# Reordering copies, maxima and low parts around the attention stages of a two-block transformer kernel

## The chip, the cores and the metric

The kernel runs on one core of a Trainium2 chip, in one launch. The metric is the device time of the program in microseconds (us); the time before is the median of three runs. A profile of one execution is read for everything else.

## The reference

Two transformer blocks run one after the other on x of 256 tokens by 2048 columns, everything in float32. What is computed, cut to what matters here:

```
mod = silu(c) @ w_ada + b_ada                 # six rows of 2048 (adaLN): shift, scale, gate, twice
h   = rms(x) * (1 + scale1) + shift1
aq, ak, av, gq, gf, gi, gg = split(h @ w_in)  # 7 parts of 1024 columns
attn = dilated attention, 8 heads of 128: rms norm and rope on q, k; three branches
       (window, dilation) = (128,1), (512,4), (2048,16), mixed by their softmax weights
hg   = gated linear recurrence on gq, gf, gi, chunks of 64, 8 heads
x    = x + gate1 * (concat(rms(attn), hg) @ w_out)
x    = x + gate2 * (square(relu(h2 @ w_ff1)) @ w_ff2)      # hidden 8192
# second block
q, k, v = split(rms(x) @ sb_w_qkv)            # 16 heads of 128, q and k rms normalised per head
z = q k^T / sqrt(128); a = exp(logsig(z) + suffix sums of logsig(-z)), strictly causal
x = x + (a v) @ sb_w_o
x = x + square(relu(rms(x) @ mlp_w_in)) @ mlp_w_out
```

## The kernel before

**Matrix products.** Each float32 operand is split into a high part of type float32r and a low part that holds the rest (`A_hi`, `A_lo` for activations, `w_hi`, `w_lo` for weights), and a product is three matmuls: hi by hi, hi by lo, lo by hi. Weights come in pieces of 1 MB (`raw`, four buffers). A block of weights is four pieces (called chunks in the code); one piece is 24 matmuls of 128x512 in `chunk` (L269 to L271): two halves of 128 tokens, four row tiles of 128, three products. SyncE (SP) issues the load of a piece, ScalarE (ACT) copies it to `w_hi` (`split_hi`, L255) once PE is done with the piece four before, VectorE (DVE) subtracts to get `w_lo` (`split_lo`, L259), and TensorE (PE) waits for `lo_rdy`. Three pairs of PSUM banks take the results; a pair is free again when its reader has counted up `pair_read`.

**Order.** No scheduler decides anything: each engine has its own list of work, in the order in which the Python code emits it, and the engines meet in semaphores only. The stages are interleaved by hand in steps: a step is one piece on PE, with the small work of the previous group (`at_stage`, `hg_stage`) and the group's own (`at_own`, `hg_own`) put beside it.

**First block, attention.** `proj_groups` gives two attention groups (four heads each, three blocks: q, k, v) and then two recurrence groups. `at_own` squares q and k on ACT, sums on DVE, takes the root on GpSimd (POOL, `power`, L642: `ssq` to the power -1/2, always eight columns wide), scales the rows on ACT (`norm_rows`, L746), rotates them on DVE, turns them on PE and copies them back on ACT as `qT` (L771) and `kT` (L776). In group 0 the q copy and the scaling of k fall into the same step, 11. `at_stage` works on one head every two steps: scores on PE, maxima on DVE (L1359, with the reciprocals of the head before, L1339), exponentials on ACT (L812, L813), the turn on PE (L1830), a copy on ACT (L822), the product with v on PE (L1843).

**adaLN sums.** In the same steps DVE adds up the later parts of `silu(c) @ w_ada` from a ring of four pieces in X (L1177, two pieces a step, `ada_slot`, L1386), and now and then collects a finished sum (L1162, L1164). SP issues the loads of the ring (L496) from the same queue as the weights, and waits for `ring_used`.

**Second block.** The last piece of the first MLP, the residual sum on DVE (`X`, L1617 and L1620, four blocks of 512 columns), the turns of X on PE (`mix_turn`), `A_hi` on ACT (L356) and `A_lo` on DVE (L375, `mix_steps`) and the first q, k pieces run into each other. DVE sums squares of X per block (`block_squares`, L975) and takes the root after the last block (`root_of_blocks`, L979, L433). Then four groups (`sb_group`) of four heads follow, the last three in a hardware loop; v is copied by ACT (L737) at step 0 of the group after. After the last group `tail` starts the output projection: it turns the six finished tiles of MIX (L320, five banks), and the last two (`LATE4`) come after piece 8. The wait for turned tiles is one per piece (`a_chunk`, L304; L2052 for piece 9), except that the first q piece has one more of its own (L2032).

**The middle.** Between output projection and MLP of the first block, each half of 128 tokens has its root (`last_half`, L1485), its scaled rows (`rows_half`, L1493), its turns (L402), A_hi (L415) and A_lo (L420).

Of the kernel before, what the change touches and what calls it, by code (L numbers as in the profile page):

```python
# [32 lines left out]
ALU = mybir.AluOpType  # L33
# [97 lines left out]
def build(nc, a, out):  # L131
    ctx = ExitStack()
    with ctx:
# [128 lines left out]
        def chunk(pe, B, j, pair, hi, lo, start, stop, between=None, tokens=range(T), half=None):  # L262

            pe.wait_ge(lo_rdy, 4 * B + j + 1)
            for t in tokens:
# [14 lines left out]
        def square_chunk(pe, B0, order, pos, take, between=None, tokens=range(T)):  # L280
# [3 lines left out]
            if pos == mine[0] and 0 in tokens:  # L284
                take(b % 3)
            return chunk(pe, B0 + pos // CH, pos % CH, pairs[b % 3], lambda i, t: A_hi[:, CH * k + i, P * t:P * t + P],
                         lambda i, t: A_lo[:, CH * k + i, P * t:P * t + P], pos == mine[0], pos == mine[-1], between, tokens=tokens)
# [13 lines left out]
        def a_chunk(pe, B, j, pair, turned=None, tokens=range(T)):  # L301

            if turned is not None:
                pe.wait_ge(a_lo, KT // 2 * turned + 2 * (j + 1))  # L304
            chunk(pe, B, j, pair, lambda k, t: A_hi[:, CH * j + k, P * t:P * t + P],
                  lambda k, t: A_lo[:, CH * j + k, P * t:P * t + P], j == 0, j == CH - 1, tokens=tokens)
# [306 lines left out]
        def _(pool):  # L613
# [25 lines left out]
            def power(i):  # L639

                pool.wait_ge(sum_rdy, i + 1)
                pool.tensor_tensor(rstd[:, :], ssq[:, :], mhalf[:, :], ALU.pow).then_inc(rstd_rdy, 1)  # L642

            for i in range(MIX_JOBS + 2):
                power(i)
# [3 lines left out]
            with pool.Fori(MIX_JOBS + 2, JOBS) as i:  # L649
                power(i)  # L650
# [3 lines left out]
        def _(act):  # L654
# [95 lines left out]
            def at_own(n, B0, s, by_row=False):  # L750
                steps = at_steps(n)
                if s in steps["norm"] and not by_row:
                    which = steps["norm"].index(s)
                    norm_rows(n, which, (QN, KN)[which])
# [9 lines left out]
                if s == steps["copy"][0]:  # L764
# [7 lines left out]
                    c.then_inc(pair_read[0], 1)  # L772
                if s == steps["copy"][1]:
# [7 lines left out]

            def at_stage(n, B0, s, stick):
                if s == 0:
                    act.wait_ge(chunk_done, 4 * (B0 + 3))
                    if not isinstance(n, int) or n:
                        act.wait_ge(pv_mm, 4 * n)
                    if stick:
                        from_pair(VN, 2, ACT.Copy, True).then_inc(pair_read[2], 1)
                    else:
                        act.activation(V1_heads[:, :, :, 0:HD], PS[:, 4:6, :].rearrange("p t (h d) -> p t h d", d=HD),  # L790
                                       ACT.Copy).then_inc(pair_read[2], 1)
# [1317 lines left out]
```

## Time and profile before

| | us |
|---|---|
| median of 3 runs | 2403.96 (2402.80 to 2404.01) |
| the profiled execution | 2404.46 |
| its span | 2402.7 |
| PE busy | 2327.9 (97%) |
| DVE busy | 1641.8 (68%) |
| ACT busy | 1047.6 (44%) |
| POOL busy | 51.4 (2%) |
| mean granted TensorE clock | 0.993 of full |

The span is the time from the first to the last instruction; what lies around it is the difference to the execution's own time. Busy time counts instructions that compute; an engine that waits for a semaphore is idle. All starts below are us from the span's start. Stages: start and adaLN to 140, attention of block 1 from 140 to 320, recurrence to 545, MLP 1 from 600 to 1270, second attention to 1650, MLP 2 to the end.

### The profile page before, as it was taken

The numbers are of one execution on the slowest core, as the hardware profiler recorded it, in microseconds if no ns is written. First come the engines' busy times: TensorE is split into PE (matmuls) and PEld (weight loads), VectorE is DVE, ScalarE is ACT, GpSimd is POOL, SyncE is SP. The second block draws the span as 40 slices with busy tenths as digits, with TensorE's granted clock in tenths as the row PEclk, the third lists the DMA queues.
The fourth block names the chain that finished last, engine by engine and source line by source line (L and its number), as shares of the span: only waits on it lengthen the run. The fifth ranks groups of instructions, "written<-read, shape, count | busy, mean of one in ns | idle before, by whom it ended". The sixth has DMA issues, their size and how long they took to land.

```text
span 2402.7 us, 27691 instructions
## 1 busy us (share of the span) xinstructions
PE 2327.9 (97%) x10698; PEld 1940.5 (81%) x10698; DVE 1641.8 (68%) x1349; ACT 1047.6 (44%) x922; POOL 51.4 (2%) x56
## 2 busy tenths in 40 slices
PE   4789999999999999999999999999999999999999
PEld 4677888887888888888887888878888888888887
DVE  7868989887677677665678456556666565665665
ACT  2245553435444343443444566564444343443442
POOL 1011000001000000000000000000000000000000
PEclk9989999999999999999999999999999999999999
DMA  9988987754877777666664545435566666666663
GB/s 351 369 293 319 352 316 265 265 205 142 293 254 271 263 263 277 230 228 206 212 213 167 197 145 170 158 129 168 190 222 224 211 227 212 211 230 210 213 228 123
DMA packets 258185, 553.86 MB, mean 231 GB/s; under 512 B 12281, under 2 KB 29122, under 8 KB 255426
## 3 DMA queue, kind: packets, MB, share of 16 engines
q1 hardware_dynamic: 257408, 552.72, 66.7%
q8 instruction: 48, 0.79, 0.1%
q10 hardware_dynamic: 706, 0.17, 0.0%
q14 instruction: 23, 0.19, 0.0%
HBM read 533.96 MB, written 18.87 MB: 230 GB/s over the span
## 4 chain that ended last, share of the span: by engine, by line
PE 89%; DVE 4%; DMA 2%; ACT 1%; issue 1%; DVEq 1%; POOL 1%; ACTq 0%; SPq 0%
PE PS L269 28%; PE PS L270 28%; PE PS L271 28%; DMA ada_raw<-in_w_ada_dram 2%; PE PS L1778 1%; DVE w_lo L259 1%; PE PS L1713 1%; DVE ada_acc L1177 1%; PE PS L320 1%; POOL rstd L642 1%; PE PS L1723 1%; ACT w_hi L255 1%; PE PS L1739 1%; DVE MS L1122 0%; PE PS L1843 0%
## 5 line engine op out<-in xcount | busy, mean ns | idle before, releaser
L259 DVE TENSOR_TENSOR w_lo<-raw,w_hi 128x2048 fp32r<-128x2048 f32 x392 | 897.2, 2290 | 540.7 <-ACT w_hi L255 535.5
L255 ACT ACTIVATE w_hi<-raw 128x2048 fp32r<-128x2048 f32 x392 | 751.3, 1917 | 1050.7 <-PE PS L271 1038.1
L269 PE MATMUL PS<-w_hi,A_hi 128*128 128x512 f32 x2112 | 837.9, 397 | 11.6 <-DVE A_lo L375 5.1
L270 PE MATMUL PS<-w_lo,A_hi 128*128 128x512 f32 x2112 | 826.5, 391 | 0.0
L271 PE MATMUL PS<-w_hi,A_lo 128*128 128x512 f32 x2112 | 826.4, 391 | 0.0
L269 PEld LDWEIGHTS PS<-w_hi,A_hi 128*128 128x128 f32 x2112 | 399.6, 189 | 94.1 <-issue 4.1
L271 PEld LDWEIGHTS PS<-w_hi,A_lo 128*128 128x128 f32 x2112 | 399.0, 189 | 84.4
L270 PEld LDWEIGHTS PS<-w_lo,A_hi 128*128 128x128 f32 x2112 | 399.5, 189 | 80.9 <-issue 1.0
L269 PE MATMUL PS<-w_hi,H_hi 128*128 128x512 f32 x1024 | 398.5, 389 | 0.4 <-DVE SQ L1617 0.4
L270 PE MATMUL PS<-w_lo,H_hi 128*128 128x512 f32 x1024 | 398.4, 389 | 0.0
L271 PE MATMUL PS<-w_hi,H_lo 128*128 128x512 f32 x1024 | 398.3, 389 | 0.0
L269 PEld LDWEIGHTS PS<-w_hi,H_hi 128*128 128x128 f32 x1024 | 192.3, 188 | 40.7 <-DVE SQ L1617 0.8
L271 PEld LDWEIGHTS PS<-w_hi,H_lo 128*128 128x128 f32 x1024 | 192.3, 188 | 39.9
L270 PEld LDWEIGHTS PS<-w_lo,H_hi 128*128 128x128 f32 x1024 | 192.3, 188 | 39.8
L1177 DVE SCALAR_TENSOR_TENSOR ada_acc<-X,sc,ada_acc 128x1024 f32<-128x1024 f32 x90 | 115.3, 1281 | 4.5
L1543 DVE TENSOR_TENSOR X<-X,PS 128x1024 f32<-128x1024 f32 x60 | 72.6, 1210 | 31.6 <-PE PS L271 31.6
L1543 DVE TENSOR_TENSOR ACC<-ACC,PS 128x1024 f32<-128x1024 f32 x60 | 72.6, 1210 | 28.4 <-PE PS L271 28.4
L642 POOL TENSOR_TENSOR rstd<-ssq,mhalf 128x8 f32<-128x8 f32 x20 | 44.7, 2235 | 1653.4 <-DVE ssq L433 1386.7
L1122 DVE SCALAR_TENSOR_TENSOR MS<-ada_raw,sc,MS 128x2048 f32<-128x2048 f32 x25 | 58.7, 2350 | 15.4 <-DMA ada_raw<-in_w_ada_dram 14.9
L899 ACT ACTIVATE H_hi<-SQ 128x512 fp32r<-128x512 f32 x64 | 36.9, 624 | 58.2 <-DMA SQ<-H_spill 58.2
L1713 PE MATMUL PS<-sc,ada_raw 128*128 128x1 f32 x160 | 29.0, 315 | 30.5 <-DMA ada_raw<-in_w_ada_dram 30.5
L1713 PEld LDWEIGHTS PS<-sc,ada_raw 128*128 128x128 f32 x160 | 28.9, 282 | 31.1 <-DMA ada_raw<-in_w_ada_dram 16.7
(268 smaller groups left out, 1096.9 us busy)
## 6 DMA issues: line engine op xcount, KB each, us to landing
raw<-in_w_ff_dram SPq DMA_DIRECT2D x128, 1024.0 KB, 5.3
raw<-in_mlp_w_in_dram SPq DMA_DIRECT2D x64, 1024.0 KB, 5.3
raw<-in_mlp_w_out_dram SPq DMA_DIRECT2D x64, 1024.0 KB, 5.1
raw<-in_w_in_dram SPq DMA_DIRECT2D x56, 1024.0 KB, 8.0
X<-in_w_ada_dram SPq DMA_DIRECT2D x96, 512.0 KB, 5.7
raw<-in_sb_w_qkv_dram SPq DMA_DIRECT2D x48, 1024.0 KB, 5.1
ada_raw<-in_w_ada_dram SPq DMA_DIRECT2D x32, 1024.0 KB, 9.9
raw<-in_w_out_dram SPq DMA_DIRECT2D x16, 1024.0 KB, 6.8
```

The source lines that it names most:

```text
L255: act.activation(w_hi[:, j, :, :], raw[:, j, :, :], ACT.Copy).then_inc(hi_rdy, 1)
L259: dve.tensor_tensor(w_lo[:, j, :, :], raw[:, j, :, :], w_hi[:, j, :, :].bitcast(F32), ALU.subtract).then_inc(lo_rdy, 1)
L269: pe.matmul(bank(pair + t), h, w_hi[:, j, k, :], start=first, stop=False)
L270: pe.matmul(bank(pair + t), h, w_lo[:, j, k, :], start=False, stop=False)
L271: mm = pe.matmul(bank(pair + t), l, w_hi[:, j, k, :], start=False, stop=last)
L320: mm = pe.transpose(bank(banks[pos % len(banks)], P * q, P * q + P), src[:, t, kt * P:kt * P + P], ident[:, :])
L642: pool.tensor_tensor(rstd[:, :], ssq[:, :], mhalf[:, :], ALU.pow).then_inc(rstd_rdy, 1)
L899: act.activation(of_token(H_hi, par, t), SQ_turned[:, t], ACT.Copy).then_inc(h_hi, 1)
L1122: ins = dve.scalar_tensor_tensor(out=MS[:, 1 - h, :], in0=sl, scalar=sc[:, k:k + 1], in1=MS[:, 1 - h, :], op0=ALU.mult, op1=ALU.add)
L1177: ins = dve.scalar_tensor_tensor(out=acc, in0=ada_ring[:, q % CH, :], scalar=sc[:, k:k + 1], in1=acc, op0=ALU.mult, op1=ALU.add)
L1543: dve.tensor_tensor(ac, ac, PS[:, b:b + 2, :], ALU.add).then_inc(acc_read, 1)
L1713: mm = pe.matmul(bank(6, at, at + 1), ada_raw[:, k % CH, P * c:P * c + P], sc[:, k:k + 1], start=True, stop=True)
```

## The change

Six edits, none of which changes what is computed.

- `chunk` takes `turned`: the piece is then computed two row tiles at a time, for both halves of tokens, and each two wait for their own count of `a_lo`. It is used for the first four q pieces and the first four MLP pieces of the second transformer block (`a_chunk`) and for piece 9 of the second output projection, in place of L2052.
- ACT in `at_own`: the scaling of rows (`norm_rows`) is emitted after the squares and the q copy of the step, not before.
- ACT in the second block: the v copy (`stick_v`) is emitted at step 11 of its own group, ahead of the k copy, not at step 0 of the next.
- DVE in the groups that follow an attention group: `ada_slot` of a step is emitted in the next step behind `at_stage`, not at its own step's end.
- DVE at the start of the second block: `mix_steps(0)` is emitted ahead of the low part of piece 1 and of X blocks 2 and 3, and `block_squares(1)` after the last `mix_steps`.
- POOL: `power` takes a width, 2 columns for six of the 20 roots (those over whole rows), 8 for the others.

```diff
+        def chunk(..., half=None, turned=None):
             pe.wait_ge(lo_rdy, 4 * B + j + 1)
+            if turned is not None:
+                for i in range(CH // 2):
+                    pe.wait_ge(a_lo, turned + i + 1)
+                    for t in range(T):
+                        for k in (2 * i, 2 * i + 1):
+                            h, l = hi(k, t), lo(k, t)
+                            first, last = start and k == 0, stop and k == CH - 1
+                            pe.matmul(bank(pair + t), h, w_hi[:, j, k, :], start=first, stop=False)
+                            pe.matmul(bank(pair + t), h, w_lo[:, j, k, :], start=False, stop=False)
+                            mm = pe.matmul(bank(pair + t), l, w_hi[:, j, k, :], start=False, stop=last)
+                return mm.then_inc(chunk_done, 1)
...
         def a_chunk(pe, B, j, pair, turned=None, tokens=range(T)):
-            if turned is not None:
-                pe.wait_ge(a_lo, KT // 2 * turned + 2 * (j + 1))
...
+                  turned=None if turned is None else KT // 2 * turned + 2 * j)
...
-            def power(i):
+            def power(i, w):
                 pool.wait_ge(sum_rdy, i + 1)
-                pool.tensor_tensor(rstd[:, :], ssq[:, :], mhalf[:, :], ALU.pow).then_inc(rstd_rdy, 1)
+                pool.tensor_tensor(rstd[:, 0:w], ssq[:, 0:w], mhalf[:, 0:w], ALU.pow).then_inc(rstd_rdy, 1)
+            by_token = (0, POWER_OF[1] - 1, MIX_JOBS, MIX_JOBS + 1)
             for i in range(MIX_JOBS + 2):
-                power(i)
+                power(i, T if i in by_token else 8)
...
-            with pool.Fori(MIX_JOBS + 2, JOBS) as i:
-                power(i)
+            power(MIX_JOBS + 2, T)
+            with pool.Fori(MIX_JOBS + 3, JOBS - 1) as i:
+                power(i, 8)
+            power(JOBS - 1, T)
...
             def at_own(n, B0, s, by_row=False):
                 steps = at_steps(n)
-                if s in steps["norm"] and not by_row:
-                    which = steps["norm"].index(s)
-                    norm_rows(n, which, (QN, KN)[which])
...
                         c = act.activation(heads_t(qT, i), bank(i), ACT.Copy, ...)
                     c.then_inc(pair_read[0], 1)
+                if s in steps["norm"] and not by_row:
+                    which = steps["norm"].index(s)
+                    norm_rows(n, which, (QN, KN)[which])
...
+            def stick_v(n, B0):
+                act.wait_ge(chunk_done, 4 * (B0 + 3))
+                act.wait_ge(pv_mm, 4 * n)
+                from_pair(VN, 2, ACT.Copy, True).then_inc(pair_read[2], 1)
...
+                    if s == 11:
+                        stick_v(AT_GROUPS + g, B0)
                     at_own(AT_GROUPS + g, B0, s, True)
...
                             at_stage(pi, s, False, None)
+                            if s:
+                                ada_slot(CH * B0 + s - 1)
...
-                    ada_slot(CH * B0 + s)
+                    if not i or groups[i - 1][0] == "hg" or s == CH * nb - 1:
+                        ada_slot(CH * B0 + s)
...
             for b in range(4):
                 cols = slice(NC_ * b, NC_ * (b + 1))
+                if b == 2:
+                    mix_steps(0)
                 if b in (1, 2):
                     split_lo(dve, QKV0, b - 1)
...
-                if b in (1, 2):
-                    block_squares(b - 1)
-                if b == 2:
-                    mix_steps(0)
+                if b == 1:
+                    block_squares(0)
             mix_steps(1)
...
-            for b in (2, 3):
+            for b in (1, 2, 3):
                 block_squares(b)
...
-            pe.wait_ge(a_lo, 5 * KT // 2)
...
-                square_chunk(pe, WO0, WO_ORDER, pos, take)
+                square_chunk(pe, WO0, WO_ORDER, pos, take, turned=4 * KT // 2 + len(EARLY4) if pos == WO_EARLY else None)
```

## Rows read from the trace of the kernel before

**Rows 1.** PE's waits, whole span: total us, times, longest us

```profile
PE PS L269 <- DVE A_lo L375: 5.1, 2, 2.9
PE PS L1830 <- ACT E L813: 3.2, 1, 3.2
PE PS L269 <- ACT qT L771: 2.4, 1, 2.4
PE PS L269 <- DVE A_lo L420: 2.1, 2, 1.7
PE PS L320 <- ACT V L737: 2.1, 1, 2.1
PE PS L1843 <- ACT AM L819: 1.8, 3, 0.6
PE PS L1811 <- issue: 1.4, 1, 1.4
PE PS L1824 <- DVE E L1349: 1.2, 3, 0.4
```

**Rows 2.** Windows: length, busy us of PE, PEld, DVE, ACT, POOL, clock, DMA

```profile
176.15:181.70 5.55, 5.55 (x24) 4.57 (x25) 5.35 (x6) 2.67 (x2) 0.00 (x0) 1.00 0.91 313
223.08:230.20 7.12, 7.12 (x27) 5.76 (x26) 6.92 (x5) 1.82 (x2) 0.00 (x0) 0.76 0.94 317
1594.26:1603.98 9.72, 9.72 (x48) 8.59 (x48) 7.25 (x17) 8.64 (x17) 0.00 (x0) 0.82 0.32 110
1659.31:1666.50 7.19, 7.19 (x24) 5.74 (x25) 2.29 (x1) 0.78 (x1) 0.00 (x0) 0.76 0.40 126
```

**Rows 3.** Timeline of ACT, step 11 of attention group 0: start, us, what, idle before

```profile
172.77 2.18 ACT L746 ACTIVATE KN<-PS,rstd 128x128 f32<-128x128 f32 x8 [3.38 <-POOL rstd L642]
174.78 1.32 ACT L771 ACTIVATE qT<-PS,w_cols 128x512 f32<-128x512 f32 x2
```

**Rows 4.** Timeline of DVE, then its groups from 176 to 323 (busy, mean ns, idle)

```profile
207.00 1.22 DVE L1297 TENSOR_REDUCE ssq<-QN 128x8 f32<-128x1024 f32 x1 [1.78 <-ACT QN L735]
217.99 2.67 DVE L1177 SCALAR_TENSOR_TENSOR ada_acc<-X,sc,ada_acc 128x1024 f32<-128x1024 f32 x2
...
L1359 DVE CUSTOM_DVE_ANT_0 E<-PS,maskadd 128x128 f32<-128x128 f32 (+1 forms) x16 | 5.1, 356 | 0.7 <-issue 0.5
```

**Rows 5.** SP's waits from 140 to 330, then a low part and its use

```profile
SPq L496 <- DVE ada_acc L1177: 127.3, 53, 6.9
...
256.59 2.29 DVE L259 TENSOR_TENSOR w_lo<-raw,w_hi 128x2048 fp32r<-128x2048 f32 x1
...
267.52 0.58 PE L269 MATMUL PS<-w_hi,A_hi 128*128 128x512 f32 x1
```

**Rows 6.** Timeline of POOL and DVE: smallest memset, roots, low part

```profile
1.38 0.10 POOL L621 MEMSET mhalf<- 128x8 f32 x1
...
577.77 2.28 DVE L259 TENSOR_TENSOR w_lo<-raw,w_hi 128x2048 fp32r<-128x2048 f32 x1
577.93 3.61 POOL L642 TENSOR_TENSOR rstd<-ssq,mhalf 128x8 f32<-128x8 f32 x1 [11.34 <-DVE ssq L1485]
...
1305.15 1.64 POOL L642 TENSOR_TENSOR rstd<-ssq,mhalf 128x8 f32<-128x8 f32 x1 [711.33 <-DVE ssq L433]
```

**Rows 7.** Timeline of ACT and DVE, start of the second block

```profile
1274.94 1.57 ACT L356 ACTIVATE A_hi<-PS,colB 128x256 fp32r<-128x256 f32 x4 [4.58 <-PE PS L320]
...
1282.68 1.66 DVE L375 SCALAR_TENSOR_TENSOR A_lo<-PS,colB,A_hi 128x256 fp32r<-128x256 f32 x4
...
1306.90 8.89 DVE L259 TENSOR_TENSOR w_lo<-raw,w_hi 128x2048 fp32r<-128x2048 f32 x4
```

**Rows 8.** Timeline of DVE, tail of the second attention and output projection

```profile
1592.98 2.29 DVE L259 TENSOR_TENSOR w_lo<-raw,w_hi 128x2048 fp32r<-128x2048 f32 x1 [5.17 <-ACT w_hi L255]
1595.80 4.79 DVE L375 SCALAR_TENSOR_TENSOR A_lo<-PS,one_c,A_hi 128x256 fp32r<-128x256 f32 x12 [0.52 <-ACT A_hi L356]
...
1657.60 1.66 DVE L375 SCALAR_TENSOR_TENSOR A_lo<-PS,one_c,A_hi 128x256 fp32r<-128x256 f32 x4 [3.17 <-ACT A_hi L356]
```

More of the change, by code:

```diff
@@ L260, in split_lo, with chunk @@
                               ALU.subtract).then_inc(lo_rdy, 1)
-        def chunk(pe, B, j, pair, hi, lo, start, stop, between=None, tokens=range(T), half=None):
+        def chunk(pe, B, j, pair, hi, lo, start, stop, between=None, tokens=range(T), half=None, turned=None):
             pe.wait_ge(lo_rdy, 4 * B + j + 1)
+            if turned is not None:
[9 more added lines that the diff above has]
+                return mm.then_inc(chunk_done, 1)
             for t in tokens:
@@ L278, in chunk, with square_chunk @@
             return mm
-        def square_chunk(pe, B0, order, pos, take, between=None, tokens=range(T)):
+        def square_chunk(pe, B0, order, pos, take, between=None, tokens=range(T), turned=None):
             b, k = order[pos]
@@ L286, in square_chunk @@
             return chunk(pe, B0 + pos // CH, pos % CH, pairs[b % 3], lambda i, t: A_hi[:, CH * k + i, P * t:P * t + P],
-                         lambda i, t: A_lo[:, CH * k + i, P * t:P * t + P], pos == mine[0], pos == mine[-1], between, tokens=tokens)
+                         lambda i, t: A_lo[:, CH * k + i, P * t:P * t + P], pos == mine[0], pos == mine[-1], between, tokens=tokens, turned=turned)
         def last_of(order, b):
@@ L301, in a_chunk @@
         def a_chunk(pe, B, j, pair, turned=None, tokens=range(T)):
-            if turned is not None:
-                pe.wait_ge(a_lo, KT // 2 * turned + 2 * (j + 1))
             chunk(pe, B, j, pair, lambda k, t: A_hi[:, CH * j + k, P * t:P * t + P],
-                  lambda k, t: A_lo[:, CH * j + k, P * t:P * t + P], j == 0, j == CH - 1, tokens=tokens)
+                  lambda k, t: A_lo[:, CH * j + k, P * t:P * t + P], j == 0, j == CH - 1, tokens=tokens,
+                  turned=None if turned is None else KT // 2 * turned + 2 * j)
         def turn_pe(pe, n, src, steps=ALL, first=0, banks=WIDE):
@@ L780, in _ @@
             AMf = AM[:, :, :, :].rearrange("p r h s -> p (r h s)")
+            def stick_v(n, B0):
+                act.wait_ge(chunk_done, 4 * (B0 + 3))
+                act.wait_ge(pv_mm, 4 * n)
+                from_pair(VN, 2, ACT.Copy, True).then_inc(pair_read[2], 1)
             def at_stage(n, B0, s, stick):
-                if s == 0:
+                if s == 0 and not stick:
                     act.wait_ge(chunk_done, 4 * (B0 + 3))
-                    if not isinstance(n, int) or n:
+                    if n:
                         act.wait_ge(pv_mm, 4 * n)
[L787 to L791, printed above, removed]
+                    act.activation(V1_heads[:, :, :, 0:HD], PS[:, 4:6, :].rearrange("p t (h d) -> p t h d", d=HD),
+                                   ACT.Copy).then_inc(pair_read[2], 1)
                 if not stick and s >= 4 and s % 2 == 0 and s <= 2 * GH + 2:
```

## The prediction

> **What bounds the kernel.** I read the busy shares first: PE (TensorE) is busy for 97% of the span, so only two things can be won: time in which PE stands still, and time in which it runs at its lower clock. Eight entries of the list of PE's waits lie in the stages that the change touches [rows 1]. Three of them (5.1, 3.2 and 2.4 us) carry most. The stage windows then show what a wait costs a second time: after three of them TensorE's granted clock falls to 1.2 GHz for some microseconds, and a block of 24 matmuls takes 7.12 and 7.19 us (mean clock 0.76) where it takes 5.55 us at 2.4 GHz [rows 2]. That is 1.6 us a time; a third such row, at 1284.6, reads the same and is not shown. So a removed wait of 3 us is worth 4.6. Last I read each wait back in order of time on the engine that ends it [rows 3 to 8].
>
> **q copied before the k rows are normalised.** In the first attention group ACT normalises k (2.18 us, held by the root until 172.77) and only then copies q at 174.78 [rows 3]. The copy frees the PSUM pair of PE's next piece, which waits 2.4 us [rows 1]. q was turned five microseconds earlier, so after the change the copy lies in the 3.38 us in which ACT sits idle before the k rows, and costs nothing; the k rows keep their time. PE needs the turned k only after its next piece (5.4 us later), and DVE is done with it 1.5 us after ACT. Gain 2.4; no new wait follows.
>
> **Maxima before the adaLN additions.** Before a head's maxima DVE makes two additions, 2.67 us, as at 217.99 [rows 4]. The wait of 3.2 us for the exponentials of head 2 hangs on a longer chain: maxima of head 1, exponentials, squares of q, their sum on DVE, the root, the q rows, their rotation, a low part, the additions, the maxima of head 2. Two pairs of additions leave it: the earlier one (2.1 us) moves into the 1.78 us in which DVE waits for the squares before 207.00 [rows 4], worth 1.7; the later one gives 2.67. Head 2 is ready 4.4 earlier; PE, 2.4 earlier by the q copy, then waits 3.2 + 2.4 - 4.4 = 1.2. Gain 2.0, and the 1.6 of the slow block, since the stop of 2.4 that ends at 176.15 is followed by a block at clock 1.00 [rows 2]. What the additions pass: the collecting of finished sums falls behind odd steps, where no maxima stand, and keeps its place; the low part of each step no longer waits behind the additions of its own step but behind those of the last, so the work between two low parts is the same. SP waits for these very additions (53 times in this stretch) before it issues the next adaLN pieces, and the weight pieces stand behind them [rows 5]; they come 0.8 later per head, the maxima's own length, while PE takes a low part 8.64 us after it is ready at the tightest place (end 258.88, use 267.52) [rows 5]. The cover holds. If DVE had to wait for scores, it would break, but before the 16 instructions of eight heads' maxima it waited 0.7 us in all [rows 4]. Stage: 2.4 + 2.0 + 1.6 = 6.0; bounds 2.4 and 7.6.
>
> **Narrower root.** Six of 20 roots shrink from 8 to 2 columns. No row has a two-column root: from 0.10 us (the smallest memset) to the 1.64 of the wide one; by columns 0.4, which I take as the nearest [rows 6]. Only two matter. The root at 577.93 takes 3.61 us: it started 0.16 after a low part, and ends 1.5 after that one does (580.05), so POOL seems shut out until then. It then gates the scaled rows at 581.58, whose chain (rows, low part, half-turn's low part) ends PE's 1.7 us wait, the larger of the two of L420 [rows 1]. Narrow, it ends before DVE is free at 580.7: gain 0.8 (0 if width costs nothing). The Trainium skill, page SBUF — State Buffer, section "SBUF: two separate sides", says that VectorE and GpSimd hold their shared port pair as an exclusive lock for a whole instruction. By that rule the 2 us before the low part's end cannot be won whatever the width, and the trace agrees (3.61 against 1.64); had the whole 3.61 scaled, the root alone would end 2.7 earlier, yet DVE's own work would still cap the gain at 0.9.
>
> **Boundary to the second block.** PE waits 2.9 us of the 5.1 for the first block's A_lo, which DVE starts at 1282.68, though A_hi of block 0 is ready at 1276.5 [rows 7]. Before it stand a low part, two X operations and two pairs of squares. Moved ahead: A_lo 1276.4 to 1278.1, low part to 1280.4, X blocks 2 and 3 to 1282.9 and 1285.5, A_lo of block 1 to 1287.2 (1288.7 before). PE starts at 1281.4 instead of 1284.6, needs no slow block, ends its piece at 1286.9, and now waits 0.3 for A_lo of block 1 before it turns block 2: 2.9 + 1.6 - 0.3 = 4.2. What is late next: three pairs of squares (4.9 us instead of 3.2) and the root now stand ahead of the low part that begins at 1306.90. By the same sums A_lo of block 3 ends at 1296.7, squares 1301.7, root 1302.9, the low part 1305.2, PE's use 1305.6 (1309.88 - 4.2 = 1305.7). It just fits; with an unchanged root it is 0.8 late. So 4.2, bounds 3.0 and 4.9.
>
> **v copied first.** In the loop over groups the v copy (1.27 us) moves into ACT's wait for the turned k, and k comes 0.35 later; both have a whole piece to spare, and the loop's remaining waits (1.8 and 1.2) hang on DVE and stay [rows 1]. Only the tail gains. There PE waits for k (1.4) and then for v (2.1) [rows 1]. The second goes, the first grows to 1.8. But A_lo, which releases the sixth turn and the next piece, starts at 1595.80 behind a low part that ends 1595.27, which itself follows k's copy [rows 8]: it does not move, and PE gets the wait back after five turns. Left are what the slow clock costs here (mean 0.82 over 9.72 us, 1.75) [rows 2] less a likely return of it: I take 0.5, bounds -0.9 and 1.2.
>
> **Half chunks.** The ninth piece of the output projection waits 2.2 us for both A_lo steps, 1.66 us together [rows 8]; after the change for the first, 0.8 less. The wait is then 1.4, short of what lowered the clock, so 1.6 more: 2.4, bounds 0.8 and 2.5. In the first q piece the finer wait does nothing, as the old one (L2032) stays, and in the last MLP none of PE's waits stood; 24 matmuls in another order cost the same.
>
> **Sum.** 6.0 + 0.8 + 4.2 + 0.5 + 2.4 = 13.9. The profiled execution took 2404.46 us (span 2402.7), 0.5 above the median 2403.96. Against it: 2404.46 - 13.9 = 2390.6; the median of runs I set at 2390.4.
>
> **Rivals.** (1) The clock still falls: the remaining stops at 218, 1595 and 1658 each keep a slow block. For it: a fall came after only 2.2 us at 1657. Against: none after 2.4 at 174 [rows 2]. Price 1.6 + 1.6 + 1.7 = 4.9: 2395.3. (2) DVE takes back what the first stage gives: from 176 to 323 it has hardly any slack, and PE now runs 6 us earlier against it. Against: the 8.64 us of cover and DVE's own waits for ACT. Price 6.0: 2396.4. Both: 2399.7, as one slow block is in both. (3) The other side: SP's queue. If DVE comes to a head's maxima before PE has scored, it waits with the additions behind it, SP with the adaLN loads, and weights behind those. At five steps of each of two groups this costs up to a pair of additions, 26.7 us; it decides once 8.64 is used up: 18.1 lost, with two slow blocks 21.3, 2411.7. Against it stands the 0.7 us of [rows 4]. (4) The change doesn't do what it says where the narrow root costs as much as the wide one and v first gives nothing: 0.8 + 0.5 + 0.8, 2392.5, inside the forecast's own range.
>
> **Numbers.** Forecast 0.70, own range 2386.5 to 2395 (the bounds above, not all at one end); (1) alone 0.13, (2) alone 0.09, both 0.04, (3) 0.04. Range 2387 to 2397.5: the upper end takes in (1) and (2) alone. 0.2% is 4.8 us, about what a measurement of this kernel tells from no change: faster below 2399.2. So faster 0.92, same 0.04, slower 0.04.
>
> **What would show it.** No wait of PE for qT; the wait for E of head 2 near 1.2 us, with its block at full clock; A_lo of block 0 before 1279 less the shift, and a wait of under 0.5 before the turn of block 2; no gap before the first k piece; the V wait gone, replaced by one inside the tail's turns; 1.4 before the ninth output piece. The prediction is wrong if low parts reach PE late between 170 and 560, or if the granted clock has as many falls as before.

## The result, and the profile after

The changed kernel takes 2390.5 us, median of 4 runs (2387.74 to 2390.72), against 2403.64 us before on the same chip: ratio 0.9944, 95% interval 0.993 to 0.9959. Forecast were 2390.4 us and a range of 2387 to 2397.5. The profiled execution took 2390.71 us, span 2388.7.

The list of PE's waits comes first, whole span (total us, times, longest us), without the rows of 4.9 us and more, which all lie in the start. Its rows answer to [rows 1]:

```profile
...
PE PS L330 <- DVE A_lo L385: 2.0, 1, 2.0
PE PS L280 <- DVE A_lo L388: 1.9, 1, 1.9
PE PS L1863 <- ACT AM L834: 1.9, 3, 0.6
PE PS L1831 <- issue: 1.7, 1, 1.7
PE PS L272 <- DVE A_lo L385: 1.5, 1, 1.5
...
PE PS L280 <- DVE A_lo L430: 1.2, 2, 0.7
PE PS L1844 <- DVE E L1366: 1.2, 3, 0.4
PE PS L1850 <- ACT E L828: 1.1, 1, 1.1
```

The waits for qT and for V are gone, the one for E at head 2 fell from 3.2 to 1.1, the one before the ninth output piece (L272) to 1.5, and the larger of the two of L430 from 1.7 to 0.7. The first row shown is new: it stands inside the tail's turns. The row marked issue, a wait for which the profile shows no cause, is the tail's wait at the scores, which the prediction puts down to k; it was 1.4 [rows 1]. The row of L388 was there before, in the start, and is not among [rows 1].

The windows of the blocks behind four of these places (same columns as [rows 2]; the clock is the third number from the end):

```profile
217.97:223.52 5.55, 5.55 (x28) 4.59 (x26) 5.18 (x5) 1.82 (x2) 0.00 (x0) 1.00 0.75 244
1273.77:1279.32 5.55, 5.55 (x27) 4.41 (x25) 5.28 (x8) 3.22 (x5) 0.00 (x0) 1.00 0.58 189
1582.39:1593.30 10.91, 8.84 (x39) 6.92 (x38) 7.80 (x17) 7.48 (x14) 0.00 (x0) 0.84 0.30 98
1646.96:1652.51 5.55, 5.55 (x25) 4.59 (x26) 2.93 (x3) 1.48 (x1) 0.00 (x0) 1.00 0.14 33
```

Three of the four slow blocks of before run at 2.4 GHz now; in the tail the clock still falls.

ACT in step 11 of group 0, answering to [rows 3], shows q copied ahead of the k rows:

```profile
168.70 1.25 ACT L781 ACTIVATE qT<-PS,w_cols 128x512 f32<-128x512 f32 x2
172.18 2.18 ACT L759 ACTIVATE KN<-PS,rstd 128x128 f32<-128x128 f32 x8 [2.23 <-POOL rstd L652]
```

DVE at the boundary and in the tail, answering to [rows 7, 8]:

```profile
1268.68 1.66 DVE L385 SCALAR_TENSOR_TENSOR A_lo<-PS,colB,A_hi 128x256 fp32r<-128x256 f32 x4
...
1287.40 1.66 DVE L385 SCALAR_TENSOR_TENSOR A_lo<-PS,colB,A_hi 128x256 fp32r<-128x256 f32 x4 [1.50 <-ACT A_hi L366]
...
1295.31 0.17 DVE L1653 COPY row_r<-rstd 128x2 f32<-128x2 f32 x1 [0.81 <-POOL rstd L652]
1295.38 8.89 DVE L259 TENSOR_TENSOR w_lo<-raw,w_hi 128x2048 fp32r<-128x2048 f32 x4
...
1581.33 2.29 DVE L259 TENSOR_TENSOR w_lo<-raw,w_hi 128x2048 fp32r<-128x2048 f32 x1 [5.46 <-ACT w_hi L255]
1583.77 4.79 DVE L385 SCALAR_TENSOR_TENSOR A_lo<-PS,one_c,A_hi 128x256 fp32r<-128x256 f32 x12
```

And the roots on POOL, with the low part on DVE that the first of them meets, answering to [rows 6]:

```profile
571.06 2.28 DVE L259 TENSOR_TENSOR w_lo<-raw,w_hi 128x2048 fp32r<-128x2048 f32 x1
...
571.22 2.67 POOL L652 TENSOR_TENSOR rstd<-ssq,mhalf 128x2 f32<-128x2 f32 x1 [12.28 <-DVE ssq L1505]
...
1294.57 0.70 POOL L652 TENSOR_TENSOR rstd<-ssq,mhalf 128x2 f32<-128x2 f32 x1 [708.40 <-DVE ssq L443]
1305.73 3.69 POOL L652 TENSOR_TENSOR rstd<-ssq,mhalf 128x8 f32<-128x8 f32 x1 [10.46 <-DVE ssq L443]
```

**The drift.** For a change of 13 us in small parts a list of waits is coarse, so the traces are set side by side in another way. PE works through 392 weight pieces of 24 matmuls each, in the same order in every kernel here. The start of a piece in one trace less its start in the trace of after is the drift, and where the drift changes, time was lost or won. The table gives, for each trace, the drift at piece 8, and then its change from stretch to stretch, in us: the copy of q (pieces 8 to 14), heads 0 to 2 (14 to 22), the root (22 to 190), the boundary (190 to 206), the loop over groups (206 to 241), its last steps (241 to 247), the tail (247 to 256), the rest; then the sum without the start.

```
kernel                  start |  8-14  14-22  22-190  190-206  206-241  241-247  247-256  256-391 | sum
before                   0.59 |  2.73   3.37    0.99     4.28    -0.02    -0.01    -0.29     2.35 | 13.42
e1_q_undone             -3.01 |  4.27  -1.64    0.00     0.05    -0.04    -0.01     0.18     0.01 |  2.83
e2_ada_undone           -0.50 |  0.00   6.13   -0.01     0.03    -0.07    -0.01     0.16     0.02 |  6.25
e3_roots_wide            1.24 |  0.00   0.00    0.94     0.97    -0.02     0.00    -1.43     0.02 |  0.49
e4_boundary_undone      -3.16 |  0.02  -0.03   -0.01     4.13    -0.11    -0.03    -1.40     0.01 |  2.59
e5_v_late               -2.29 |  0.01  -0.03    0.03     0.04     0.00    -0.03     0.35    -0.01 |  0.37
e6_piece9_whole         -2.00 |  0.01   0.01    0.00     0.05    -0.08    -0.02     0.03     0.72 |  0.72
e7_tail_first           -0.67 |  0.01  -0.06    0.03     0.03     0.06     0.56    -0.59     0.01 |  0.05
e8_three_orders          1.28 |  0.02  -0.03    0.01     0.07    11.82    -0.26    -0.58     0.01 | 11.05
e9_subtract_ahead        0.05 |  0.01   0.01    0.00     0.09    -1.76    -0.87    -1.43     0.00 | -3.95
e10_head0_ahead         -1.44 |  0.00   0.01    0.04     0.05    -3.81    -0.85    -1.43     0.00 | -6.00
e11_all_orders          -0.11 |  0.00   0.01    0.04     0.05    -3.75    -0.61    -2.35     0.01 | -6.59
e12_same_again          -1.62 |  0.00   0.00   -0.01     0.09    -0.03     0.02     0.10     0.00 |  0.17
```

A stretch that an edit does not touch repeats to 0.1 us. Two things do not repeat: the start, before piece 8, whose drift lies anywhere in 4.4 us from one execution to the next, and falls of the clock, 1.4 to 1.7 us each. The runs' times carry both, so the single edits are read from the drift and the times only bear them out.

### The profile page after: what moved, and what is told of

Read it like the earlier page. It is cut to its first block, busy times and chain, and to the rows that moved or that the text cites. A ratio compares the mean times of both kernels' runs of the same rounds, so it can differ in the third digit from the quotient of the medians.

```text
span 2388.7 us, 27685 instructions
## 1 busy us (share of the span) xinstructions
PE 2324.8 (97%) x10698; PEld 1937.2 (81%) x10698; DVE 1642.0 (69%) x1349; ACT 1047.8 (44%) x922; POOL 47.8 (2%) x56
## 4 chain that ended last, share of the span: by engine, by line
PE 90%; DVE 4%; DMA 2%; ACT 1%; DVEq 1%; issue 1%; POOL 0%; ACTq 0%; SPq 0%
PE PS L280 27%; PE PS L282 27%; PE PS L281 27%; DMA ada_raw<-in_w_ada_dram 2%; PE PS L1798 1%; DVE w_lo L259 1%; PE PS L1733 1%; PE PS L272 1%; PE PS L274 1%; PE PS L273 1%; PE PS L330 1%; DVE ada_acc L1194 1%; ACT w_hi L255 1%; PE PS L1743 1%; PE PS L1759 0%
## 5 line engine op out<-in xcount | busy, mean ns | idle before, releaser
L280 PE MATMUL PS<-w_hi,A_hi 128*128 128x512 f32 x2040 | 809.2, 397 | 3.1 <-DVE A_lo L388 1.9
L282 PE MATMUL PS<-w_hi,A_lo 128*128 128x512 f32 x2040 | 798.2, 391 | 0.0
L281 PE MATMUL PS<-w_lo,A_hi 128*128 128x512 f32 x2040 | 797.7, 391 | 0.0
L280 PEld LDWEIGHTS PS<-w_hi,A_hi 128*128 128x128 f32 x2040 | 385.9, 189 | 82.6 <-DVE A_lo L388 2.0
L282 PEld LDWEIGHTS PS<-w_hi,A_lo 128*128 128x128 f32 x2040 | 385.0, 189 | 81.5
L281 PEld LDWEIGHTS PS<-w_lo,A_hi 128*128 128x128 f32 x2040 | 386.0, 189 | 78.4 <-issue 1.0
L652 POOL TENSOR_TENSOR rstd<-ssq,mhalf 128x8 f32<-128x8 f32 (+1 forms) x20 | 41.1, 2056 | 1642.0 <-DVE ssq L443 1377.9
```

The source lines that it names most:

```text
L280: pe.matmul(bank(pair + t), h, w_hi[:, j, k, :], start=first, stop=False)
L281: pe.matmul(bank(pair + t), h, w_lo[:, j, k, :], start=False, stop=False)
L282: mm = pe.matmul(bank(pair + t), l, w_hi[:, j, k, :], start=False, stop=last)
L652: pool.tensor_tensor(rstd[:, 0:w], ssq[:, 0:w], mhalf[:, 0:w], ALU.pow).then_inc(rstd_rdy, 1)
```

## The experiments

Ratios are to the kernel before, with 95% intervals; each kernel is the changed one with the edit shown.

**1. The q copy behind the k rows again.**

```diff
+                if s in steps["norm"] and not by_row:
+                    which = steps["norm"].index(s)
+                    norm_rows(n, which, (QN, KN)[which])
                 if s == steps["square"][0]:
...
                     c.then_inc(pair_read[0], 1)
-                if s in steps["norm"] and not by_row:
-                    which = steps["norm"].index(s)
-                    norm_rows(n, which, (QN, KN)[which])
```

> The changed kernel (2390.5 us) with the q copy behind the normalisation of k again in the first attention stage; all else of the change stays. Interplay theory (mine): the order of q sets when head 0 of the first group starts, but from head 2 on DVE's maxima and collections decide. At piece 12 of the drift the 2.6 us come back, of which head 2's wait (1.1 us in the changed kernel, 3.0 before) gives back what it can spare: net 1.2 us lost, 2391.7, and the clock fall at 127.6 stays away or is moved. Additive rival: q's 2.4 to 2.6 us are lost in full: 2393.0, and if the clock falls again as before, 2394.6.

Measured 2391.13 us, 0.9949 (0.9929 to 0.9968); one of its four runs, 6063 us, lies far outside, and without it the median is 2390.45. PE's waits from 160 to 240 us and the window behind them:

```profile
PE PS L280 <- ACT qT L784: 2.4, 1, 2.4
```

```profile
172.53:179.72 7.19, 7.19 (x25) 5.79 (x26) 6.99 (x6) 2.65 (x2) 0.00 (x0) 0.76 0.86 292
```

The wait for qT is back and the one for E at head 2 is gone: PE comes there late enough. From piece to piece (12, 13, 17, 19) the drift changes by +2.57, +1.69, -0.35 and -1.31. The 1.69 are the clock, which fell right behind this wait, so the order of q by itself is worth 2.57 - 0.35 - 1.31 = 0.9, near the 1.2 of the interplay; the additive rival's 2.4 to 2.6 are out. The fall itself neither theory foresaw: in the kernel before, PE waited as long at this place and the block behind ran at clock 1.00 [rows 2]. The fall at 127.6 that the expectation names is one of the start's, which every trace has.

**2. The maxima behind the additions again.**

```diff
                             at_stage(pi, s, False, None)
-                            if s:
-                                ada_slot(CH * B0 + s - 1)
...
-                    if not i or groups[i - 1][0] == "hg" or s == CH * nb - 1:
-                        ada_slot(CH * B0 + s)
+                    ada_slot(CH * B0 + s)
```

> The changed kernel with only the order of the maxima undone: in the first attention stage the pieces of ada's sums stand ahead of the next head's work on DVE again. Interplay theory: head 2 of the first group is then late whatever q does, so q's gain is lost with it (its wait at head 2 grows by what the wait at head 0 gave) and the clock falls as before: 2.1 + 2.6 + 1.6 = about 6.0 us lost, 2396.5; the drift against the kernel before then falls by 2.6 at weight piece 12 and climbs back at piece 19. Additive rival: only its own 2.0 and the clock's 1.6 are lost: 2394.1.

Measured 2395.07 us, 0.9968 (0.9957 to 0.9978). PE's waits from 170 to 240 us, and the window behind the longest:

```profile
PE PS L1847 <- ACT E L828: 5.5, 3, 3.8
```

```profile
221.98:229.17 7.19, 7.19 (x28) 5.77 (x27) 6.97 (x5) 1.82 (x2) 0.00 (x0) 0.76 0.98 328
```

All of the first stage's gain is lost, 6.13 us against 6.10 (2.73 + 3.37) for both edits undone. With DVE late at three heads (the drift rises by 1.42, 0.34 and 2.74, then 1.62 for the clock) the early q copy is worth nothing. The additive rival (3.6) is out.

**3. All roots over eight columns.**

```diff
-                power(i, T if i in by_token else 8)
+                power(i, 8)
...
-            power(MIX_JOBS + 2, T)
+            power(MIX_JOBS + 2, 8)
...
-            power(JOBS - 1, T)
+            power(JOBS - 1, 8)
```

> The changed kernel with all roots of GpSimd over eight columns again. Theory: the loss is the 0.9 us of the root at 571 us (piece 74 of the drift) and nothing elsewhere, since the boundary's own root at 1294.6 us (0.70 us now) is followed by work that the DVE has in hand only in part: 0 to 0.9 there. 2391.4, up to 2392.3. Rival: the span of a root is set by how it meets the low parts on the shared port, so the width is worth nothing on the path: 2390.5.

Measured 2391.0 us, 0.995 (0.9933 to 0.9967). PE's waits from 500 to 1310 us, two of the roots on POOL, and the tail's window in this trace:

```profile
PE PS L280 <- DVE A_lo L430: 2.2, 2, 1.7
PE PS L280 <- DVE w_lo L259: 0.9, 1, 0.9
```

```profile
572.46 3.62 POOL L652 TENSOR_TENSOR rstd<-ssq,mhalf 128x8 f32<-128x8 f32 x1 [11.34 <-DVE ssq L1505]
...
1296.78 1.64 POOL L652 TENSOR_TENSOR rstd<-ssq,mhalf 128x8 f32<-128x8 f32 x1 [708.44 <-DVE ssq L443]
```

```profile
1585.52:1595.01 9.49, 7.33 (x40) 5.88 (x38) 7.80 (x17) 7.48 (x14) 0.00 (x0) 1.00 0.33 112
```

The width is worth 0.94 at the middle root and 0.97 at the boundary, 1.9 in all, where the reordered squares leave no room for a wide root. That is just over the 0 to 0.9 that the theory gave the boundary, and the rival's nothing is out. And where the clock fell in the tail of the changed kernel (0.84 over 10.91 us) it did not here (1.00 over 9.49 us), with the same work and the same 2.0 us of waiting: 1.4 us to the good that have nothing to do with roots.

**4. The boundary's order undone.**

```diff
-                if b == 2:
-                    mix_steps(0)
                 if b in (1, 2):
                     split_lo(dve, QKV0, b - 1)
...
-                if b == 1:
-                    block_squares(0)
+                if b in (1, 2):
+                    block_squares(b - 1)
+                if b == 2:
+                    mix_steps(0)
...
-            for b in (1, 2, 3):
+            for b in (2, 3):
```

> The changed kernel with the order of the turn and the squares at the boundary to the second block undone. Theory: the terms are independent of all else, so 4.3 us come back at weight pieces 200 and 201, with the clock fall at 1284.7: 2394.8. Rival: the narrower root and the earlier v have moved the place, and less than 3 us come back: below 2393.5.

Measured 2391.7 us, 0.9956 (0.9939 to 0.9972). PE's waits from 1260 to 1290 us and the window behind:

```profile
PE PS L272 <- DVE A_lo L385: 2.7, 1, 2.7
```

```profile
1273.57:1280.75 7.18, 7.18 (x25) 5.71 (x26) 6.39 (x7) 0.22 (x1) 0.00 (x0) 0.76 0.01 2
```

4.13 us come back at this place (2.98 + 1.38 - 0.23), of 4.28. The finer waits of the q pieces were not undone by themselves; what is left for them here is 0.15. The time rose by only 1.2: the start was 3.2 earlier than in the trace of after, and the clock did not fall in the tail (-1.40). Read by its time alone this run would have spoken for the rival.

**5. v copied late again.**

```diff
                 at_stage(n, B0, 0, stick)          # in tail
+                if stick:
+                    stick_v(n, B0)
...
+                        if s == 0:
+                            stick_v(AT_GROUPS + g - 1, B0 - 3)
                         at_stage(AT_GROUPS + g - 1, B0 - 3, s, True)
-                    if s == 11:
-                        stick_v(AT_GROUPS + g, B0)
```

> The changed kernel with v's copy back at the head of the next stage (and of the tail's turn) in the second block's attention; all else of the change stays. Theory: v first does nothing that the path sees; in the tail the wait at E's use of v (1.9 us before) comes back in place of the waits inside the turns, so against the changed kernel the drift at pieces 248 and 249 shows between -0.3 and +0.6 us and the clock falls or not in either: 2390.2 to 2391.0. Rival (my forecast's step): v first was worth 0.5 us, with up to 0.5 more per stage in the loop: 2391.0 to 2392.5.

Measured 2389.43 us, 0.9944 (0.993 to 0.9957). PE's waits from 1570 to 1600 us:

```profile
PE PS L330 <- ACT V L750: 2.1, 1, 2.1
PE PS L1833 <- issue: 1.4, 1, 1.4
PE PS L1846 <- DVE E L1368: 0.6, 1, 0.6
```

The wait for V is back in place of the one inside the turns, and the loop's stretches do not move (0.00, -0.03). In the tail this trace is 0.35 longer than after, while the trace of before was 0.29 shorter; a fall of the clock lies in all three, at another point of the work each time. The edit is worth nothing that can be told from zero.

**6. The ninth output piece waits for both low parts again.**

```diff
+            pe.wait_ge(a_lo, 5 * KT // 2)
             def mlp_turn(b):
...
-                square_chunk(pe, WO0, WO_ORDER, pos, take, turned=4 * KT // 2 + len(EARLY4) if pos == WO_EARLY else None)
+                square_chunk(pe, WO0, WO_ORDER, pos, take)
```

> The changed kernel with the half chunk undone: the tensor engine waits for the low parts of both last turned blocks before piece 9 of the output projection. Theory: 0.8 us of waiting comes back at piece 257 of the drift (0.70 measured there in the change), and with a wait that long (2.6 us) the clock falls again, 1.6 us more: 2392.9. Rival: the two are not bound together, the clock falls or doesn't whatever this wait is, as it did at 1585 us in the changed kernel and not in two of its variants: 0.8 us alone, 2391.3.

Measured 2389.96 us, 0.9942 (0.9929 to 0.9956). PE's waits from 1640 to 1660 us and the window behind:

```profile
PE PS L280 <- DVE A_lo L385: 2.2, 1, 2.2
```

```profile
1645.65:1651.20 5.55, 5.55 (x24) 4.62 (x25) 2.29 (x1) 0.79 (x1) 0.00 (x0) 1.00 0.22 52
```

The wait is as long as before, and the clock stays up: 0.72 us, the rival's answer. The 1.6 us of clock that the change won here are not bound to this wait.

**7. The tail's last weight piece split behind the turned blocks.** The last group is written out, so that it can differ.

```diff
             def tail(...):   # ScalarE; VectorE alike with split_lo
                 turn_act(act, turn, g, steps=steps, banks=TAIL)
+                if stick:
+                    split_hi(act, B, CH - 1)
...
-                    split_hi(act, B0 + s // CH + 1, s % CH)
+                    if s < 11 or not last:
+                        split_hi(act, B0 + s // CH + 1, s % CH)
...
-            with act.Fori(1, SB_GROUPS) as g:
+            with act.Fori(1, SB_GROUPS - 1) as g:
                 sb_group(g, False)
+            sb_group(SB_GROUPS - 1, False, True)
```

> The changed kernel with the last group of the second block's attention written out, and in it the last weight piece of the output projection split into high and low part only after the tail's turned blocks, on ScalarE and VectorE. Theory: in the tail the tensor engine waits 2.0 + 1.9 us at the turned blocks because VectorE does a low part of weights (1581.3, 2.3 us with what is around it) ahead of the turned ones, which are late by that; moved behind them, 2.1 us go at pieces 248 and 249, and with the wait short the clock has less cause to fall there (1.6 more where it does): 2388.4, or 2386.8. Rival: ScalarE's high parts of the turned blocks set the pace and the low part only fills what would be idle: under 0.5 us, 2390.3.

Measured 2389.99 us, 0.9945 (0.9931 to 0.9958). PE's waits from 1570 to 1600 us:

```profile
PE PS L1852 <- DVE E L1370: 2.5, 1, 2.5
PE PS L1839 <- issue: 1.7, 1, 1.7
```

The wait inside the turns is gone, and head 0's E takes its place with 2.5 us, since the high part now stands ahead of its exponentials. The run kept the clock up in the tail, worth 1.4, and yet won only 0.59 there, and it lost 0.56 at piece 242, early in the group that is now written out. Both theories are wrong: mine missed the next in the queue, the rival the reason.

**8. The same, with two orders moved in the loop.** ScalarE does head 0's exponentials ahead of the high part of the piece at step 1; VectorE subtracts head 3's argument while it waits for k's root.

```diff
-                        at_stage(AT_GROUPS + g - 1, B0 - 3, s, True)
+                        at_stage(AT_GROUPS + g - 1, B0 - 3, s, True, True)
+                        if s == 1:
+                            exps(AT_GROUPS + g - 1, 0)
...
                 def meanwhile():
                     split_lo(dve, B0 + s // CH + 1, s % CH)
+                    if ahead and s == 8:
+                        subtract(n - 1, 3)
```

> The kernel of the run before this one, and in the three groups of the second block's attention stages ScalarE does head 0's exponentials ahead of the weight piece's high part, and VectorE subtracts head 3's argument while it waits for the root of k's squares. Theory: the wait of E's matmul at head 0 in the loop goes down by the high part's 0.55 us and that of the product with v at head 3 by 0.79 us, three times each: 4.0 us off, 2384.4 with the tail's 2.1. Rival: those waits are short of cover elsewhere (the low part or the root then comes late and the next chunk waits): under 1 us off, 2387.8, or slower than the run before.

Measured 2403.1 us, 0.9994 (0.9985 to 1.0003): 11.8 us lost in the loop. PE's waits from 1300 to 1570 us, then ACT and DVE in the first of three such places, and the window behind it:

```profile
PE PS L1865 <- DVE E L1383: 10.5, 3, 3.5
```

```profile
1358.75 0.62 ACT L806 ACTIVATE E<-E,one_c 128x384 f32<-128x384 f32 x1
1359.27 1.90 ACT L255 ACTIVATE w_hi<-raw 128x2048 fp32r<-128x2048 f32 x1
...
1361.20 2.29 DVE L259 TENSOR_TENSOR w_lo<-raw,w_hi 128x2048 fp32r<-128x2048 f32 x1 [6.74 <-ACT w_hi L255]
1363.69 0.56 DVE L1378 SCALAR_TENSOR_TENSOR E<-PS,E 128x384 f32<-128x384 f32 x1 [0.19 <-issue]
```

```profile
1365.00:1370.00 5.00, 4.72 (x19) 4.19 (x20) 3.41 (x4) 0.53 (x1) 0.00 (x0) 0.69 0.67 211
```

The exponentials were ready at 1359.4, 1.1 us earlier than in the changed kernel once the start is taken off. But DVE stood 6.74 us at the low part, whose high part came behind them, with E's work queued behind it. One engine's order was changed and the other's not. The 4.5 us that each group loses here are 3.1 of waiting (3.5 where the changed kernel waits 0.4) and 1.4 of clock, which fell behind all three waits. At the same time the drift fell by about 0.9 at each of pieces 222, 234 and 246, which speaks for the subtraction.

**9. Only the subtraction moved.** (The second edit of the last diff.)

> The changed kernel with one order moved: in the three groups of the second block's attention stages VectorE subtracts head 3's argument while it waits for the root of k's squares, not after the normalisation of k. Theory: the product with v at head 3 waited 0.79 us for it in each of the three groups; the three-orders run fell by 0.88, 0.89 and 0.85 us at these pieces (222, 234, 246) although its time as a whole rose. Alone it gives 2.6 us: 2387.8 against 2390.4. Rival: in that run these falls only gave back a part of what the late exponentials had cost just before (a wait that shrinks because the engine comes later); alone it is worth under 0.5 us.

Measured 2385.07 us, 0.9923 (0.9909 to 0.9936). The drift falls by 0.87, 0.88 and 0.89 at the three pieces, 2.6 us, as the theory has it, and PE's wait for AM is no longer in its list. The rest of the 3.95 is the tail's clock (1.43), up in this trace, less 0.1 spread over the other stretches.

**10. Both queues in the new order.**

```diff
# ScalarE
-                    if not first:
-                        at_stage(AT_GROUPS + g - 1, B0 - 3, s, True)
+                    if not first and s != 2:
+                        at_stage(AT_GROUPS + g - 1, B0 - 3, s + (s == 1), True)
# VectorE
-                    if not first:
-                        at_stage(AT_GROUPS + g - 1, s, True, sb_cols(g - 1))
+                    if not first and s != 2:
+                        at_stage(AT_GROUPS + g - 1, s + (s == 1), True, sb_cols(g - 1), True)
```

> The run before this one, and head 0's exponentials ahead of the weight piece's high part on ScalarE, this time with VectorE's work on them ahead of that piece's low part too. Theory of why the three-orders run lost 4.0 to 4.5 us per group: the high part came behind the exponentials, and VectorE, whose next instruction was the low part of it, stood still until then, with E's maxima and minima queued behind. With both queues in the new order the wait at E's matmul (0.55 us per group) goes: 1.6 us less, 2386.2. Rival: the loss was ScalarE's own, the exponentials hold it until the next piece and everything behind is late: then 2 us or more per group are lost here as well, above 2394.

Measured 2385.47 us, 0.9925 (0.9912 to 0.9939). ACT and DVE at the same place:

```profile
1356.59 1.91 ACT L255 ACTIVATE w_hi<-raw 128x2048 fp32r<-128x2048 f32 x1
...
1356.71 0.56 DVE L1368 SCALAR_TENSOR_TENSOR E<-PS,E 128x384 f32<-128x384 f32 x1 [4.93 <-ACT E L823]
...
1358.75 4.59 DVE L259 TENSOR_TENSOR w_lo<-raw,w_hi 128x2048 fp32r<-128x2048 f32 x2 [0.16 <-issue]
```

PE's wait for E in the loop is gone, and the drift falls by a further 0.66 at each of pieces 215, 227 and 239. So the loss of experiment 8 was DVE's order and nothing of ScalarE's. The medians of 9 and 10 don't show these 2.0 us (the start and the clock move them by more); their traces do.

**11. With the tail's piece behind head 0's exponentials.**

```diff
                     at_stage(n, B0, s, stick)
+                    if stick and s == 2:
+                        split_hi(act, B, CH - 1)
```

> The run before this one with the last group written out again and the last piece's high and low part split behind head 0's exponentials in the tail, not between the turned blocks and them. Theory: the turned blocks' wait of 2.2 us goes as in the tail-first run; the 2.7 us that E's matmul waited there in its place shrink by the high part's 1.1 and the low part's share to about 1.1; leaving the loop early costs 0.7 as there; 0.7 less in all than the run before, 2385.5, and 1.5 less where the clock stays up at this place and falls there otherwise. Rival: E's matmul waits for a chain that starts at the turned blocks on ScalarE whatever is behind it, 2.0 us or more: no gain, 2386.5.

Measured 2383.57 us, 0.9917 (0.9903 to 0.9931), the fastest here: 5.7 us under the changed kernel on the same chip (experiment 12). PE's waits from 1300 to 1600 us:

```profile
PE PS L1846 <- issue: 1.7, 1, 1.7
PE PS L1859 <- DVE E L1377: 0.7, 1, 0.7
PE PS L1878 <- ACT AM L834: 0.2, 1, 0.2
```

E's matmul now waits 0.7 where it waited 2.5 in experiment 7. In the tail this trace is 0.92 shorter than experiment 10's, with the clock up in both; the group written out costs 0.24 and the loop's other pieces 0.06, so 0.6 is left, as the theory's 0.7 has it.

**12. The changed kernel again.**

> The changed kernel itself once more, on the same chip as the three runs before, to read them against it: 2390.3 by its earlier runs. In the earlier variants with the same waits as it to 0.01 us at the tail's turned blocks (2.2 us) the clock fell there in some and not in others. If the fall is a matter of how the execution as a whole lies in time, this trace may show it or not, with 1.5 us at piece 249 of the drift; if it belonged to the place, it shows it at 1585 us again.

Measured 2389.26 us, 0.9943 (0.9929 to 0.9956). The clock fell at 1584 us, in the same weight piece as in the first trace (the drift at piece 249 does not move). One repeat doesn't decide it. Of nine traces with these same turns and the same 2.0 us of waiting (the changed kernel's two, experiments 1 to 4, 6, 9 and 10) five have the fall and four have not.

## Why the prediction was right

Each step against the drift (stretches of the row "before"):

- **First attention stage**: forecast 6.0, measured 2.73 + 3.37 = 6.10. PE waits 1.1 for E at head 2 where 1.2 were forecast, and the block behind is at full clock. The sum stands, its split does not. I booked 2.4 to the copy of q and 3.6 to the maxima. Undone one at a time they cost 0.9 (with the fall of the clock taken off) and 6.1: the step "head 2 is ready 4.4 earlier; PE, 2.4 earlier by the q copy, then waits 1.2" already said that the two are not additive, and the booking forgot it.
- **Narrower root**: forecast 0.8 in the middle, measured 0.94 to 0.99. The guess of 0.4 us for two columns was low, 0.70, inside its bounds. The size of the guess hardly matters in the middle, for most of the root's span there is the low part's: begun at 571.06, that ends at 573.34, and the root 0.55 later (571.22 + 2.67); the wide root of experiment 3 ended 1.5 after its low part, as in [rows 6]. The Trainium skill, page SBUF — State Buffer, section "SBUF: two separate sides", has VectorE or GpSimd, whichever starts first, hold the shared port pair for a whole instruction. The trace agrees: 0.70 alone and 2.67 behind a low part, 1.64 and 3.6 for the wide one.
- **Boundary**: forecast 4.2, measured 4.28, and in reverse 4.13. The times of the chain came out. Moved by the 7.7 us that the kernel is already ahead there (0.59 + 2.73 + 3.37 + 0.99), the forecast has block 3's A_lo end at 1289.0 (1289.06), the root at 1295.2 (1295.27), the low part at 1297.5 (1297.67) and PE's use at 1298.0 (1297.81). "It just fits; with an unchanged root it is 0.8 late": the wide root was 0.97 late. So the root's width is worth 1.9 us in the changed kernel, and the boundary's 4.2 hold only with it. The sum is not quite that of its own times: by them PE starts 3.2 earlier (1284.6 to 1281.4), not 2.9, which makes 4.5; the drift has 3.15 and 1.37 at pieces 200 and 201 and loses 0.2 again at the next few.
- **v first**: forecast 0.5, measured -0.29, while undoing it costs 0.35, each with a fall of the clock at another point: nothing that can be told from zero. The working said that PE's own waits give nothing (A_lo behind a low part doesn't move, PE gets the wait back after five turns), and so it was: 1.7 for k where 1.8 was forecast, and 2.0 inside the turns in place of the 2.1 for V. The term that failed is what it still credited, the slow clock of the tail: a fall came again at 1585.
- **Half chunk**: forecast 2.4, measured 2.35; 0.7 of it is the wait (experiment 6 gives 0.72 back) and 1.6 the clock. The amount is right and the reason of its larger part is not. I argued that a wait of 1.4 is "short of what lowered the clock"; the full 2.2 us did not lower it in experiment 6. Whether the shorter wait makes a fall rarer was not tried.

The sum was 13.9 and the drift gives 13.42. With the start's 0.59 that is 14.0, the difference of the two spans; the profiled executions' times (2404.46 and 2390.71) differ by 13.75, as 0.25 lies outside the spans.

**The rivals.** (2), that DVE takes back the first stage, is out: the drift does not move between pieces 22 and 190 but for the root. (3) is out: SP's waits for the additions from 140 to 330 us, as in [rows 5], did not grow in sum (148.1 before, 146.6 after: the four behind the first additions of a slice went from 20.8 to 22.5 us, these from 127.3 down), and DVE waited 0.3 us before the 16 instructions of the maxima where it had waited 0.7 [rows 4]:

```profile
SPq L506 <- DVE ada_acc L1194: 124.1, 54, 5.9
```

(4) is half true (v first), and inside the forecast's own range. (1), that the clock still falls, happened at one of its three places. Its price of 4.9 counts 1.7 for the tail, where the forecast had credited only 0.5: 3.7, or 2394.1, was the price against the forecast. It is the one with a true core: the falls behind waits of 2 to 3 us are partly chance, and I treated them as fixed to the length of the wait. The forecast counted three of them, 1.6 each, as won for good, and a part of a fourth. Against the trace of before, with one fall left, it came out even; another execution can lie 1.4 us lower or higher from this alone, and 4 us from its start.

## What to carry to other kernels

Two edits that bring work forward to the same late wait (here the q copy and the maxima, 0.9 and 6.1 one at a time, 6.1 together) are not worth their sum: follow the chain to the place where it is needed, and test each edit alone. When an instruction is moved ahead on one engine, look at the head of every queue that feeds on what it passed, and move the two together; moved alone, the exponentials cost 4.5 us per group (1.4 of it clock), moved together with DVE's half they won 0.7. Line up two traces piece by piece before believing a difference of times of 1 to 3 us.

## What the runs showed of the hardware that was not expected

- **The clock's falls repeat by place only in part.** The same wait of 2.4 us for qT was followed by a block at clock 1.00 in the kernel before and at 0.76 in experiment 1; the ninth output piece's 2.2 us at 0.76 before and at 1.00 in experiment 6; the tail's 2.0 us by a lowered clock in five traces (0.84 in the trace of after) and by 1.00 in four. The waits of 2.7 to 3.8 us at the boundary and for E had a fall behind them all seven times (the kernel before twice, experiments 2 and 4, and the three of experiment 8); E's wait of 2.5 in experiment 7 had none. The Trainium skill, page TensorE: Matmul & The Clock Gate, Part 1, calls the count of slow matmuls at a kernel's start variable between runs of one kernel, since the monitor runs on its own time; no run here shows its cause, but the same variability shows in mid-kernel. Whether a start shifted on purpose would move a fall was not tried.
- **A root of two columns takes 0.70 us, one of eight 1.64**: by these two, 0.39 us and 0.16 per column.
- **A wide root of 3.69 us at 1305.73** stands where one of 1.64 stood before (1317.25), as it now begins 0.1 after a low part. DVE idles 1.53 us for it; PE, for which the low parts of the next two pieces lie ready by then, does not: its list of waits from 1262 to 1330 us names none.
- **Leaving the loop for a written-out group** cost 0.6 us at piece 242 in experiments 7 and 8 and 0.2 in experiment 11; the cause is open.
